# A streaming-encoder block in fp32 on one core: the first downward FFN stage by seven products instead of eight, its weight sums built in DRAM

## What is computed

```python
ada = (silu(c) @ w_ada + b_ada).reshape(b, 3, 3, 1024)
shift, scale, gate = ada[:, :, 0], ada[:, :, 1], ada[:, :, 2]

h = rmsnorm(x, g_ffn1) * (1 + scale0) + shift0
x = x + 0.5 * gate0 * swiglu(h, w_ffn1_up, w_ffn1_down)
h = rmsnorm(x, g_mix) * (1 + scale1) + shift1
x = x + gate1 * mixer(h)
h = rmsnorm(x, g_ffn2) * (1 + scale2) + shift2
x = x + 0.5 * gate2 * swiglu(h, w_ffn2_up, w_ffn2_down)
return rmsnorm(x, g_final)

def swiglu(h, w_up, w_down):
    g, u = split(h @ w_up, 2)
    return (silu(g) * u) @ w_down
```

## Time and profile before

| what | value |
|---|---|
| median of three runs | 1070.68 us (1070.48 to 1071.17) |
| the profiled execution, its time | 1069.39 us |
| its span, first to last instruction | 1067.6 us |
| mean granted TensorE clock | 0.998 |
| PE, DVE, ACT, POOL busy | 98%, 67%, 50%, 5% |
| DMA moved | 223.08 MB, 209 GB/s on the mean |
| chain that ended last | 90% on PE |

### The profile page before, as it was taken

How to read it: one execution, slowest core, us unless ns; L and a number is a source line. 1 busy time by engine, 2 the same in 40 slices (tenths; PEclk the granted TensorE clock), 3 DMA queues, 4 the chain that set the end, 5 groups by cost and what they waited for, 6 DMA issues and landing times.

```text
span 1067.6 us, 17029 instructions
## 1 busy us (share of the span) xinstructions
PE 1051.3 (98%) x6432; PEld 918.2 (86%) x6432; DVE 718.0 (67%) x1064; ACT 533.2 (50%) x871; POOL 57.0 (5%) x92
## 2 busy tenths in 40 slices
PE   8999999999999999999999999999999999999997
PEld 5788888888888889889878877889999999999997
DVE  5745555555554547886876676579876676689873
ACT  6422322322322225775787577448645545566653
POOL 1000000000000001211111011000000000000000
PEclk9999999999999999999999999999999999999999
DMA  9878888896598784798699867425999799967652
GB/s 341 254 228 284 265 274 291 273 305 183 154 307 222 197 257 116 137 218 211 155 198 191 185 168 156 140 80 139 236 236 227 226 259 229 211 171 204 190 163 80
DMA packets 250433, 223.08 MB, mean 209 GB/s; under 512 B 6924, under 2 KB 222588, under 8 KB 248316
## 3 DMA queue, kind: packets, MB, share of 16 engines
q1 hardware_dynamic: 233776, 154.45, 50.6%
q0 software_dynamic: 16128, 67.11, 25.7%
q10 hardware_dynamic: 460, 0.58, 0.2%
HBM read 217.93 MB, written 67.11 MB: 267 GB/s over the span
## 4 chain that ended last, share of the span: by engine, by line
PE 90%; ACT 3%; SPq 3%; DVE 2%; issue 1%; DMA 1%; ACTq 0%; DVEq 0%
PE bank L982 28%; PE bank L984 28%; PE bank L983 28%; SPq L858 2%; PE bank L1348 1%; PE bank L1320 1%; DMA w_raw<-in_w_ffn_up_dram 1%; PE bank L1296 1%; PE bank L1297 1%; PE bank L1025 1%; ACT w_hi L1539 0%; ACT tmp_b L1929 0%; DVE pt_lo L2677 0%; PE bank L1490 0%; PE bank L1298 0%
## 5 line engine op out<-in xcount | busy, mean ns | idle before, releaser
L982 PE MATMUL bank<-h_hi,w_hi 128*128 128x512 f32 (+1 forms) x592 | 230.5, 389 | 0.0
L984 PE MATMUL bank<-h_hi,w_lo 128*128 128x512 f32 (+1 forms) x592 | 223.5, 378 | 0.0
L983 PE MATMUL bank<-h_lo,w_hi 128*128 128x512 f32 (+1 forms) x592 | 223.5, 377 | 0.0
L2085 DVE TENSOR_TENSOR w_lo<-w_raw,w_hi 128x1024 fp32r<-128x1024 f32 x97 | 118.7, 1225 | 152.7 <-ACT w_hi L1539 152.1
L1539 ACT ACTIVATE w_hi<-w_raw 128x1024 fp32r<-128x1024 f32 x97 | 102.5, 1057 | 200.9 <-PE bank L984 191.5
L982 PEld LDWEIGHTS bank<-h_hi,w_hi 128*128 128x128 f32 x592 | 111.8, 189 | 24.5 <-issue 2.6
L983 PEld LDWEIGHTS bank<-h_lo,w_hi 128*128 128x128 f32 x592 | 111.7, 189 | 24.3 <-issue 3.1
L984 PEld LDWEIGHTS bank<-h_hi,w_lo 128*128 128x128 f32 x592 | 111.6, 189 | 22.6
L2245 DVE TENSOR_TENSOR up_lo<-up_raw,up_hi 128x1024 fp32r<-128x1024 f32 x80 | 86.6, 1086 | 21.0 <-ACT up_hi L1638 21.0
L984 PE MATMUL bank<-combo,up_lo 128*128 128x256 f32 x320 | 90.6, 283 | 0.0
L982 PE MATMUL bank<-combo,up_hi 128*128 128x256 f32 x320 | 90.5, 283 | 0.0
(11 more groups left out here) (293 smaller groups left out, 2267.4 us busy)
## 6 DMA issues: line engine op xcount, KB each, us to landing
w_sums<-in_w_ffn_up_dram POOLq DMA_DIRECT2D x24, 1280.0 KB, 8.6
ada_w<-in_w_ada_dram SPq DMA_DIRECT2D x56, 512.0 KB, 4.4
w_raw<-in_w_ffn_up_dram SPq DMA_DIRECT2D x48, 512.0 KB, 6.9
up_raw<-w_sums SPq DMA_DIRECT2D x40, 512.0 KB, 6.0
d_sums<-in_w_ffn_down_dram POOLq DMA_DIRECT2D x12, 1408.0 KB, 9.2
w_raw<-in_w_in_dram SPq DMA_DIRECT2D x28, 512.0 KB, 5.8
d_raw<-d_sums SPq DMA_DIRECT2D x16, 704.0 KB, 4.7
w_sums<-w_sums POOLq DMA_DIRECT2D x8, 1280.0 KB, 10.4
```

Source lines behind the costliest of these rows:

```text
L982: mm(dst, wh, xh, start=start, stop=False, skip_group_check=skip)
L983: mm(dst, wh, xl, start=False, stop=False, skip_group_check=skip)
L984: return mm(dst, wl, xh, start=False, stop=stop, skip_group_check=skip)
L2085: v.tensor_tensor(w_lo[:, s, :], w_raw[:, r, :], w_hi[:, s, :].bitcast(F32), ALU.subtract)\
```

## The change

The first downward stage takes the scheme of the second one. In order:

- `DOWN_PARTS`, `hid_hi`, `hid_lo`, `hidden_high` and `hidden_low` go. The hidden matrix of the first FFN is kept in float32 (`hid1`), and its quarters and their sums are split for each product (`moving_high`, `moving_low`, `moving_sum`).
- A second set of weight sums in DRAM for the first downward weights: 16 more pieces of 1408 KB. Twelve are issued in the first upward stage, from its tile 4 on every 13/5 tiles; four in the downward stage. Of `w_sums`, 2 pieces are issued in the upward stage, 4 in the downward one, 26 in the mixer; the 16 pieces for the second downward stage all come after them (3 at once, 11 in the second upward stage, 2 in the second downward one).
- Coefficient blocks 7 and 8 move to the upward stage: 56 products in 20 steps (`ADA_SHARES`: 4, 4, then 3, 3, 2), and its loops are unrolled.
- Seven raw and four high buffers for the weight chunks of this stage (six and five in the second).
- Squares for the mixer's norm are taken by quarters of `xT` as they become final (`square_quarter`, `fold_quarter`), the last four chunks one by one (`square_last`, `fold_last`). The sum for the left half stands after chunk 1 of the seventh product, the sum for the right half after k = 2 of the mixer's first tiles instead of k = 3.
- The mixer's first four weight tiles are loaded when the seventh product has begun.

```diff
-DOWN_PARTS = ((0, 8), (8, 8), (16, 6))
-D_RAW, D_HI = 6, 5
+D_RAW, D_HI = (7, 6), (4, 5)
+SQUARED = {(P6, 2): "x11", (P4, 2): "x22", (P3, 0): "x21"}
-UP_BLOCKS = (FC - 2) // 4
-DOWN_CHUNKS = (3, 3, 2, 0)
+ADA_SHARES = (4, 4) + (3, 3, 2) * 6
-T_MIX = T_DOWN1 + 3 * KC
+T_MIX = T_DOWN1 + N_DOWN
...
# POOL
-            for r in range(4):
-                copied_after(T_UP1 + 4 + 12 * r // 5)
-                one_piece(sums_rows(S1, r), pieces_rows(up_a, r), False)
...
+            for n, piece in enumerate(DOWN_PIECES[:12]):
+                copied_after(T_UP1 + 4 + 13 * n // 5)
+                down_piece(0, *piece)
+            for n in range(2):
+                copied_after(T_UP1 + 36 + 3 * n)
+                up_pieces(1)
+            for n, piece in enumerate(DOWN_PIECES[12:]):
+                copied_after(T_DOWN1 + 1 + 3 * n)
+                down_piece(0, *piece)
+            for n in range(4):
+                copied_after(T_DOWN1 + 13 + 3 * n)
+                up_pieces(1)
...
+            up_pieces(2)
             for j in range(1, JOBS):
                 repeat_k(j)
+                up_pieces((3, 4, 3, 2, 5, 2, 5)[j - 1])
+            for n, piece in enumerate(DOWN_PIECES):
+                if n >= 3:
+                    copied_after(T_DOWN2 + 1 + 4 * (n - 14) if n >= 14 else uses(SEVEN0 + 1 + 3 * (n - 3) // 2, 3))
+                down_piece(1, *piece)
...
# SP
+            for f in range(2, FC):
+                load_up(0, T_UP1, f, f % 2)
+                if f > 2:
+                    load_share(f - 1)
+            load_share(FC - 1)
...
+            for t in range(N_DOWN):
+                load_down(0, t)
+            def load_mix(t, dst, src):
+                if t < T_MIX + RAW:
+                    sp.wait_ge(w_used, T_DOWN1 + 25 + (t - T_MIX) // 2)
+                load_w(t, t % RAW, dst, src)
...
# PE
+            for i in (P1, P5, P2, P6, P7, P4, P3):
+                for n in range(4):
+                    down_chunk(0, i, n)
+                    if (i, n) == (P3, 1):
+                        side_sum(1, 0, 2)
...
-                if k == 3:
-                    side_sum(1, 1, 2)
+                if k == 2:
+                    side_sum(1, 1, 4)
...
# DVE
+            for f in range(2, FC):
+                share = ADA_SHARES[f - 2]
+                for half in range(2):
+                    one_product()
+                    if f < FC - 1:
+                        split_lo(T_UP1 + 2 * f + half + SPLIT, half, (2 * (f % 2) + half + SPLIT) % RAW)
+                    elif half == 0:
+                        down_low(0, 0)
+                for _ in range(share - 2):
+                    one_product()
+                if 17 <= f < 20:
+                    moving_low(0, P1, f - 17)
+                elif f == FC - 2:
+                    for j in range(3):
+                        moving_sum(0, P5, j)
+                elif f == FC - 1:
...
+                    moving_low(0, P5, 0)
+                    moving_low(0, P5, 1)
+                    down_low(0, 1)
+                hidden_first(f)
+                if products[0] % KC == 0:
+                    ada_sum(B_LOOP + blocks_made[0], 5 + blocks_made[0])
+                    blocks_made[0] += 1
...
             coefficients(1)
-            side_square_added(1, 0)
-            low_apart(1, w7_hi, w7_lo)
+            last_update(0, 0)
+            last_update(0, 1)
             side_normed(1, 0, 0)
...
+            fold_last(0)
+            fold_last(1)
+            low_apart(0, w6_hi, w6_lo)
...
+            last_update(0, 3)
+            low_apart(1, w7_hi, w7_lo)
+            fold_last(2)
+            fold_last(3)
```

More of the change, by code:

```diff
@@ L647, in product_bank @@
[L647 to L663, removed]
-            last = n if (i, n) in ((P3, 2), (P3, 3)) else n | 1
-            return T_DOWN2 + 4 * i + last + 1
+        t_down = (T_DOWN1, T_DOWN2)
@@ L668, in turn_place, with x_quarter @@
+        def x_quarter(where):
+            k0, h = x_part[where]
+            return xT[:, k0:k0 + 4, side(h)]
         def turn_place(tb, half):
@@ L771, in down_piece, with up_pieces @@
+            begun = [0]
+            def up_pieces(count):
+                for name, src, r, add in upward[begun[0]:begun[0] + count]:
+                    one_piece(sums_rows(name, r), sums_rows(src, r) if src in (S1, S2) else pieces_rows(src, r), add)
+                begun[0] += count
+            down_rows = [w.rearrange("o k n -> (o k) n") for w in (w_ffn1_down, w_ffn2_down)]
+            def down_piece(e, name, k_half, c_half, half, add):
                 pool.wait_ge(sums_made, 16 * pieces[0])
@@ L881, in _ @@
             sp.wait_ge(ada_mul, 2 * KC)
[L882 to L895 removed]
+            products = [0]
@@ new lines, in square_last @@
+            def square_last(n):
+                act.wait_ge(x_upd, last_added(0, n + 1))
+                act.wait_ge(sq_folded, 1)
+                a(sq_late[:, n, :], xT[:, n, side(1)], ACT.Square).then_inc(sq_done, 1)
+            act.wait_ge(gacc_done, 2)
+            for i in (P1, P5, P2, P6, P7, P4, P3):
+                for n in range(4):
+                    if P1 < i < P3:
+                        for j in HIGH_STEPS[n]:
+                            moving_high(0, i + 1, j)
+                    if n % 2 == 0 and (i or n):
+                        done = i if n else i - 1
+                        for m in range(2):
+                            for part, entry in enumerate(SETS):
+                                if entry[0] == done:
+                                    keep_out(0, part, 2 - n + m)
+                    if 4 * i + n + LEAD < N_DOWN:
+                        down_high(0, 4 * i + n + LEAD)
+                    if (i, n) in SQUARED:
+                        where = SQUARED[i, n]
+                        square_quarter(where, added(0, {"x11": 4, "x22": 6, "x21": 7}[where]))
```

713 lines of the change are left out of this document (350 added, 363 removed).

## The result

The changed kernel took a median of 1100.09 us (four runs, 1088.08 to 1104.65), beside 1070.58 us (1069.36 to 1071.17) for the kernel before in runs taken together with it: a ratio of 1.024, 95% interval 1.0157 to 1.0323. The run of 1104.65 us was in a slower state, and the ratio, which compares means, leaves it out. The prediction was 1063.6 us and faster; it is slower, by 29.5 us between the medians and by 25.7 by the ratio's means.

The account below looks back on a forecast made before the run. The prediction took TensorE, by number and rate of matmuls, to bound the kernel. Its terms, -14.6 + 1.5 + 1.5 + 4 + 0.5 = -7.1 us, took the median of 1070.68 to 1063.6 us; range 1057.2 to 1071.5.

Parts of the forecast that it names:

- The products: First downward stage: 924 matmuls of 256 columns at 118.9 ns each, two ada turns moved out; 14.6 us less.
- The entry of the downward stage: The last upward step must also fit DVE's preparation of the first downward product; 1.5 us lost, least 0, most about 5.
- The entry of the mixer: Left norm hidden under the last product, right half tighter at its side sum; 1.5 us lost, least 0, most 3.5.
- The first upward stage: Added transfers need 242 us of DMA engine time in 229, late in bursts; 4 us lost, least 0, most 17.
- Rival 2: First upward stage becomes DMA-bound, deciding below a carried share of about 1.02; +17 us there, 1076 in all; chance 0.12.
- Later stages: More POOL pieces in the mixer and second upward stage; 0.5 us lost, least 0, most 3.
- Rival 1: Nothing is given back: adds slow rather than loads, the two entries cost 1.5 us together; 1057.6 us, chance 0.26.

Follow-up runs that it names:

- e3: The changed kernel with a third ada buffer (4 KB per partition), two early loads held back: 1071.74 us, ratio 1.0019.
- e1: The changed kernel with its 16 pieces of sums for the first downward stage shrunk to 32 KB each: 1075.37 us, ratio 1.0046.
- e2: The changed kernel with the six adding pieces issued in the first upward stage made plain copies of the same size: 1084.25 us, ratio 1.0145.
- e8: The changed kernel itself measured once more, on the chip of e5 to e7: 1094.65 us, ratio 1.0236.
- e9: e7 with two copies of w_sums moved from the first upward stage to the mixer: 1062.49 us, ratio 0.9934.
- e10: e9 with the ada turn back at its place in the changed kernel, right behind the step: 1065.51 us, ratio 0.9955.
- e11: The changed kernel with the earlier ada schedule, two products per step, two coefficient blocks left out: 1061.5 us, ratio 0.9906.
- e4: The changed kernel with the ada turn, and VectorE's sum with it, half a step later on the queue: 1094.94 us, ratio 1.0251.
- e7: e6 plus two adds released later in the second downward stage and POOL's mixer pieces shared out anew: 1061.0 us, ratio 0.9907.
- e6: The changed kernel with three ada buffers and the ada turn half a step later: 1068.0 us, ratio 0.9985.
- e5: e3 with the last two adding pieces of the second downward stage released 7 chunks later: 1067.16 us, ratio 0.9973.

## Why the prediction was wrong

**The products** (14.6 us less). Right. The stage lasts 112.1 us in the changed kernel, with no wait and a granted clock of 0.98 (0.57 in its first 4 us, behind the last turn's wait), and 110.7 in e3; 110.1 was forecast. The rate of 118.9 ns, taken from the second downward stage, held (110.7 us for 924 matmuls is 119.8 ns, side sum included), and not the 109.2 ns that one would estimate from the isolated gap of N/2.4 + 2.5 ns, which the Trainium skill's page "TensorE: Matmul & The Clock Gate" gives in "Back-to-back issue gap".

**The entry of the downward stage** (1.5, 0 to 5). Within its bounds, at more than twice its size: the 3.3 us ahead of the last turn, 3.2 to 3.4 in e1, e2 and e8 as well. The prediction named its form, a late ada load in front of it all, and gave it too little. With three buffers e9 and e10 lose 1.3 and 1.4 us at e_lo instead; e11 loses nothing. **The entry of the mixer** (1.5, 0 to 3.5). Right: 0.9 us, at the side sum of the right half.

**The first upward stage** (4, 0 to 17). This is the step that failed. The stage ends 34.1 us late, twice the upper bound, or 30.8 without the 3.3 of the entry: 15.6 us are late ada loads and 0.2 a late weight, 5.0 are order at the first turn, and what is left, 10.0, is the clock. The DMA need was right: 242 us forecast, 244 measured. Four things went wrong.
- The loads were sized at 4 us, and 15.6 came. The step asked what landing would be allowed on the mean (7.3 us), and found only the pairs of adds above it; waits came at five turns over the whole stage. The 17 us for a step at a landing of 10 us hold for a step of three products; at the mean of 2.67 it is 15.1, so that sum leaned to the high side and still came out short.
- VectorE's order was not walked through for the first two steps, which have four products each. It costs 5.0 us at the first turn whatever the loads do (e3, e10). It was put at nothing, and the places where TensorE would wait were looked for at the conversions of weights and not at the turn. The loads are tightest there too: 8 products in 22.9 us are 2.86 each, which two buffers give only with landings near 4.4 us (two times 2.86, less 1.3), and the first turn waits 4 us more in the changed kernel than in e3.
- The 6 us of slack ahead of a TensorE wait were taken from VectorE's idle half. VectorE works in order and shares that order between ada products and weights, so time it stands at a load is not slack: e4 shows the same stall come out at w_lo. With two buffers no load can be asked for ahead to make up lateness; e3 gives one buffer more and takes away 18.8 of 23.9 us, the 15.6 of late loads and the 3.3 of the entry.
- The clock was not priced at all. The 10.0 us are a difference, 34.1 less 24.1 of waits; PE's busy time in the stage, longer by as much, agrees.

**Rival 2** (the stage becomes DMA-bound, 1076) had the sign and the place, by a mechanism that the runs refute: it was to decide below a carried share of 1.02, and at 1.00 and 1.01 e3 and e7 wait 5.1 us (all of it order) and 2.7 us in the stage; e6 carries 1.03 and waits 1.5. Its price, +17, was also half of what came. The engines ran at 0.92 because they were not asked, not because they were full.

**Later stages** (0.5, 0 to 3). Wrong too: without the 0.9 of the mixer's entry, 9.7 us. I had counted POOL's pieces there but given no price to the two adds that stand right behind the start of the second downward stage, where only four chunks are loaded ahead: 4.2 us at d_lo, 4.7 in the stage (e5 takes them away). In the mixer TensorE waits 4.7 us for k_hh loads, 0.3 before; with the clock 5.9 for the stretch. I had seen that repeat_k stands between pieces and took "an idle queue" for no cost, when an add issued 3 us ahead (642.32, for a repeat at 645.52) is still under way. In e5 and e7 the stretch from the mixer to the seven products of the second upward stage is only 0.8 us longer than before.

**Rival 1** (1057.6, nothing is given back) is what the change is worth once the stalls are repaired, less 3.4 us: 1061.0 for e7.

What stays open: which of a piece's properties hurts a landing (bytes, the add's reading back, or its small packets); only adds against copies was tried. And why the split of the stall varies between runs of one kernel. Nor was the schedule tried with the four-product steps alone changed.

## What to carry to other kernels

When work moves into a stage, don't hold its mean rate against its mean supply: take the step with the largest share, divide it by the buffers, and ask for one landing and one operation per buffer. Then write down each engine's order in that step: what stands behind the waiting instruction, and how much work lies between the last thing that TensorE releases and the next thing that it needs. Here that was 5 us, and no load had a part in it. When TensorE stalls beside DMA engines that are not full, add a request in flight before removing traffic or moving the consumer: against the second measurement of the changed kernel a third buffer of 4 KB gave 23 us, the removal of this stage's pieces of sums 19, a later consumer nothing as long as loads were late, and 3 once they were not. And when background transfers are put near the start of a stage, count how many loads are ahead there, not how many buffers the stage has.

## What the runs showed of the hardware

**A gap costs more than its length.** Around the first turn of e3, with its wait of 5.05 us, windows of 4 us on PE alone (stretch, length, busy, granted clock, DMA share, GB/s):

```profile
76.00:80.00 4.00, 3.21 (x14) 1.00 0.95 321
80.00:84.00 4.00, 0.00 (x0) 0.69 1.11 309
84.00:88.00 4.00, 3.73 (x13) 0.50 0.89 265
88.00:92.00 4.00, 4.00 (x18) 0.96 1.03 313
92.00:96.00 4.00, 4.00 (x19) 1.00 0.46 100
```

TensorE comes back at a granted clock of 0.50, the lower level of 1.2 GHz, and runs at it for some 4 us: 13 matmuls in a window that has 18 or 19 otherwise. The whole stall cost 7.4 us for 5.1 of wait. The first turn of the changed kernel (8.97 us) has the same level for the 4 us after it:

```profile
84.00:88.00 4.00, 0.00 (x0) 0.50 0.91 269
88.00:92.00 4.00, 3.33 (x12) 0.50 1.13 353
92.00:96.00 4.00, 4.00 (x16) 0.83 0.62 178
```

In 4 us windows that begin with the turn itself, the clock is 0.50 after the wait of 4.1 us, 0.62 after 4.2, 0.57 after 2.1, 0.66 after 3.3 and 1.00 after 1.2. So the length of the wait alone does not set it. The Trainium skill, page "TensorE: Matmul & The Clock Gate", section "Part 1: The HAM clock gate", says that "the default state is throttled, and activity releases the throttle". The trace agrees, and it shows the price: six waits of 23.9 us together cost 34.

**An add holds up the loads beside it more than a copy does.** With six adds made into copies the stage needs 25 us less of 16-engine time (219 for 244 us; 27 by the rows of before), and its turn waits fall by 10.0 us. Beside the add at the entry of the second downward stage four loads took 15.4 us in the median and 18.1 at most, where the stage's median is 5.0.

**An issue can take as long as a landing.** SyncE's DMA instructions last 0.34 us as a rule (ada_w, median); from 986.4 to 1006.3 us, at the adds, four d_raw issues follow each other, with a median of 4.9 us each and 7.6 for the longest. While one lasts, nothing behind it on the queue is issued.
